# High and low parts of small operands stacked at partitions 0 and 32 of one matmul

## The chip, the core and the metric

The program runs on one core of one Trainium2 chip. The metric is device time in microseconds, the median of three runs. Engines: PE (TensorE, matmuls; PEld is its weight load), DVE (VectorE), ACT (ScalarE), POOL (GpSimd) and SP (SyncE, which only issues DMAs here).

## What is computed

One decoder layer for a prompt of 512 tokens and for 8 sample rows of one token each, in fp32. Cut to what matters here:

```python
h  = rms_norm(x, norm_g) * (1 + scale) + shift                 # modulated by c
aq, ak, av, az, mqk, mv, mo, mz, mif, ga, gm = split_columns(h @ w_in)
ya = attend(aq, ak, av)          # samples: top-3 of 8 past key blocks of a paged cache, plus the new row
# mLSTM, per head (4 heads): b = cumsum(logf), d = b_t - b_s + i_s
m_t = maximum(b + m0, max_s d)                                 # running maximum, the stabiliser
w   = exp(d - m_t);  s = (q @ k.T) * w;  num = s @ v;  C, n = new matrix memory
# samples, per row: C_new = a*C + v k^T, num = C_new q, with q, k = silu(conv(mqk))
u  = sigmoid(ga) * ((ya * silu(az)) @ w_att) + sigmoid(gm) * ((ym * silu(mz)) @ w_mlstm)
y  = rms_norm(x + gate * (u @ w_out), final_g)
```

## The kernel before

Matmuls in full fp32 are slow on PE, so the kernel splits operands into a **high part** (the value as a rounded fp32r copy) and a **low part** (the value less its high part) and multiplies with fp32r matmuls. For the large products (`ztile`, L544 to L565) a weight tile of 128 columns arrives by DMA (`wraw`), ACT makes the high part (`high`, L1022), POOL the low part (`low`, L1519), and PE runs three products for each of 8 contraction steps and 2 halves of 260 columns: high by high, high by low, low by high. A tile is 48 matmuls.

The stages in order: modulation and normalisation (to about 54 us); attention, four pairs of heads in a loop, in which SP loads the samples' key pages, DVE and POOL multiply them with spread queries and DVE sums them; the choice of blocks for the samples (about 245 to 275 us); four mLSTM heads of 8 tiles each, with value pages between; the gate tiles (`T_GATE`) with the samples' state update; the output products.

Each engine runs its own program in order; semaphores (`wait_ge`, `then_inc`) join them. Nothing is scheduled by a tool: the order is as written. Four places of the program matter below, in all of which a few rows are spread over all 128 partitions by a matmul with a selector (a stationary matrix of rows that are all ones or all zeros):

- **Query copy** (`query_copy`, L684 to L688). The samples' queries (8 rows, 512 columns) lie in `qsr`, high parts in columns 0 to 511 and low parts in the next 512, both on partitions 0 to 7. Two fp32r matmuls with the selector `selc` accumulate. ACT makes the rounded copy (L1118) and a plain copy `qsN` (L1119), POOL the difference (`query_low`, L1558). ACT copies the result out (`copy_out`, L1168), which waits in the loop until DVE has freed all pages. Eight of these, two for each pair of heads.
- **Spread of the running maxima** (`spread_max`, L763 to L767). `MR` has 4 rows (heads) of 512 tokens. One matmul of plain fp32 operands with the selector `selm` (fp32, written by ACT, L1250 and L1276) spreads one head's row; in the trace each is two rows. ACT takes exponentials of the result (`decays`, L1273 to L1278). Four of these, one per head. `MR` comes from a transposition of `ec` (L733), a copy and a scan along the tokens on DVE (L1793, L1794).
- **Spread of the samples' keys and queries** (`key_query`, L923 to L934). `kqr` holds 1024 high and 1024 low columns on partitions 0 to 7, and four fp32r matmuls per sample accumulate into two banks. It comes from transpositions of `cvS` (L899), ACT's copies (L1372, L1373, L1378) and a subtraction on DVE (L2088). DVE writes the selector `selg`. Eight samples.
- **The choice of blocks** on DVE (L1924 to L1961): first two convolutions for head 0 (L1901, L1904), then comparisons of block sums up to a penalty matrix (L1941), which PE spreads (L877), and sums that PE spreads again (L791), after which head 0's maxima are spread.

Of the kernel before, what the change touches and what calls it, by code (L numbers as in the profile page):

```python
# [87 lines left out]
def decoder_step(nc, I, O):  # L88
# [14 lines left out]
    with ExitStack() as ctx:  # L103
        names = set()

        def sb(name, shape, dt=F32):
# [121 lines left out]
        selm = work(P)[0:MH, :]  # L228
# [149 lines left out]
        def _(sp):  # L378
# [161 lines left out]
        def _(pe):  # L540
# [357 lines left out]
            for k in range(KT):  # L898
                last = tr(ps[0:B, 4 + k // 4, (k % 4) * P:(k % 4 + 1) * P], cvS[:, (k + 4) % KT, :], ident[:, :])  # L899
# [112 lines left out]
        def _(act):  # L1012
# [237 lines left out]
            f(selm, rowsel[0:MH, 0, :], ACT.Copy).then_inc(selm_rdy, 1)  # L1250
# [20 lines left out]
            def decays(h, first):  # L1271
# [4 lines left out]
                f(selm, chunk(rowsel[0:MH], h + 1), ACT.Copy).then_inc(selm_rdy, 1)  # L1276
# [81 lines left out]
            f(cvS[:, :, :], cvS[:, :, :], ACT.Silu).then_inc(sam_act, 1)  # L1358
# [336 lines left out]
        def _(dve):  # L1695
# [75 lines left out]
            def gates_in():  # L1771
# [14 lines left out]
            def gate_sums():  # L1786
                dve.wait_ge(g_pe, 1)
                chain(v.tensor_copy(bc[:, :, :].rearrange("p j h -> p (j h)"), ps[:, 7, 0:16]))
                tt(ec[:, :, :], G[:, 0:TT, 0:MH], bc[:, :, :], ALU.subtract).then_inc(g_dve, 1)

            def gate_max():
                dve.wait_ge(g_pe, 2)
                chain(v.tensor_copy(eR, ps[0:MH, 7, :]))  # L1793
# [213 lines left out]
            def samples_joined():  # L2007
# [267 lines left out]
```

## Time and profile before

| | |
|---|---|
| three runs | 717.66, 722.49, 724.09 us, median 722.49 |
| span of the profiled execution | 725.2 us (2.7 us over the median; its own time is not listed apart from its span) |
| PE busy | 687.4 us, 95% |
| POOL, DVE, ACT busy | 433.6, 472.8, 333.6 us |
| mean granted clock of PE | 0.971 |

A stretch's rows are read so: start and length in microseconds, then engine, line of the kernel, operation, output and inputs with shapes, a count where several run one behind the other, and in brackets how long the engine idled before and what ended that. A matmul's length reaches to its modelled end, so lengths of neighbouring matmuls overlap, and what one occupies is the distance between starts. The granted clock is 1.00 at 2.4 GHz and 0.50 at 1.2 GHz.

### The profile page before, as it was taken

What the parts mean: (1) busy time and instruction counts of PE and PEld (TensorE: products, weight loads), DVE (VectorE), ACT (ScalarE), POOL (GpSimd) and SP (SyncE); (2) the same over time, 40 slices, a digit from 0 to 9 for tenths busy, and PEclk for the clock granted to TensorE, in tenths of its full rate; (3) what the DMA queues carried; (4) which work ended last, traced back from release to release, by engine and by line L of the source; (5) the groups of instructions that cost most, each with busy time, mean ns of one, the idle gap of its engine ahead of it and who ended that gap; (6) DMA issues with size and microseconds to landing.
All of it is one profiled execution on the core that took longest, in us unless ns stands there. A gap on an engine that the chain in (4) does not pass through costs nothing.

```text
span 725.2 us, 14754 instructions
## 1 busy us (share of the span) xinstructions
PE 687.4 (95%) x5012; PEld 611.9 (84%) x5012; DVE 472.8 (65%) x483; ACT 333.6 (46%) x726; POOL 433.6 (60%) x289
## 2 busy tenths in 40 slices
PE   1899999999999899999999999999999999999996
PEld 0577788888779668999999999997999999999974
DVE  0535489897999963995697686775555358444435
ACT  5545556547381335464464534632322224323643
POOL 4203365596687317699679688771864657666510
PEclk9997999989999978999999999999899999999999
DMA  8988349889898867287777667766675355833302
GB/s 311 343 250 248 111 123 272 267 260 274 233 304 260 269 205 233 80 248 208 228 212 230 183 189 231 226 205 192 161 198 150 101 167 167 263 88 87 88 30 89
DMA packets 156905, 144.72 MB, mean 200 GB/s; under 512 B 7548, under 2 KB 115153, under 8 KB 156853
## 3 DMA queue, kind: packets, MB, share of 16 engines
q1 hardware_dynamic: 142984, 137.15, 63.1%
q10 hardware_dynamic: 13876, 7.02, 3.3%
q8 instruction: 23, 0.38, 0.2%
q14 instruction: 22, 0.17, 0.1%
HBM read 135.10 MB, written 9.11 MB: 199 GB/s over the span
## 4 chain that ended last, share of the span: by engine, by line
PE 62%; issue 10%; POOL 9%; DVE 8%; ACT 4%; DMA 4%; SPq 2%; ACTq 0%; POOLq 0%; DVEq 0%
PE ps L556 44%; POOL sb_arenaA L1566 4%; POOL sb_wL L1519 4%; PE ps L992 3%; PE ps L822 2%; POOL sb_arenaA L1600 1%; PE ps L932 1%; DVE sb_arenaA L1838 1%; PE ps L590 1%; PE ps L783 1%; DMA sb_arenaA<-in_w_ada 1%; DVE sb_arenaB L1986 1%; DMA sb_arenaB<-in_x_sample 1%; DVE sb_arenaA L1981 1%; SPq L398 1%
## 5 line engine op out<-in xcount | busy, mean ns | idle before, releaser
L1519 POOL TENSOR_TENSOR sb_wL<-sb_wraw,sb_wH 128x512 fp32r<-128x512 f32 (+1 forms) x168 | 217.7, 1312 | 188.5 <-ACT sb_wH L1022 170.5
L556 PE MATMUL ps<-sb_hH,sb_wH 128*128 128x260 f32 x1152 | 242.0, 292 | 3.6 <-POOL sb_wL L1519 3.0
L556 PE MATMUL ps<-sb_hH,sb_wL 128*128 128x260 f32 x1152 | 235.6, 287 | 0.0
L556 PE MATMUL ps<-sb_hL,sb_wH 128*128 128x260 f32 x1152 | 235.3, 286 | 0.0
L556 PEld LDWEIGHTS ps<-sb_hH,sb_wH 128*128 128x128 f32 x1152 | 181.7, 193 | 19.6 <-issue 14.7
L1022 ACT ACTIVATE sb_wH<-sb_wraw 128x512 fp32r<-128x512 f32 (+1 forms) x168 | 99.3, 612 | 191.1 <-PE ps L556 150.5
L556 PEld LDWEIGHTS ps<-sb_hL,sb_wH 128*128 128x128 f32 x1152 | 181.5, 193 | 0.0
L556 PEld LDWEIGHTS ps<-sb_hH,sb_wL 128*128 128x128 f32 x1152 | 181.2, 192 | 0.0
L1600 POOL TENSOR_TENSOR sb_arenaA<-sb_arenaA 128x2048 f32<-128x2048 f32 x28 | 101.5, 3628 | 2.0 <-DMA sb_arenaA<-in_cache_v 2.0
L1566 POOL TENSOR_TENSOR sb_arenaA<-sb_arenaA 128x1024 f32<-128x1024 f32 x22 | 61.7, 2823 | 35.3 <-DMA sb_arenaA<-in_cache_k 35.3
L1842 DVE TENSOR_REDUCE sb_arenaA<-sb_arenaA 128x2048 f32 (+1 forms) x32 | 73.0, 2284 | 3.7 <-DVE sb_arenaA L1838 2.0
L1838 DVE TENSOR_TENSOR sb_arenaA<-sb_arenaA 128x2048 f32<-128x2048 f32 x21 | 53.9, 2565 | 6.8 <-DMA sb_arenaA<-in_cache_k 5.8
L1981 DVE TENSOR_REDUCE sb_arenaA<-sb_arenaA 128x512 f32<-128x4096 f32 x7 | 53.6, 7656 | 0.3 <-POOL sb_arenaA L1600 0.3
L1986 DVE TENSOR_REDUCE sb_arenaA<-sb_arenaA 128x512 f32<-128x4608 f32 x4 | 34.3, 8583 | 0.0
L1027 ACT ACTIVATE sb_arenaB<-ps 128x520 f32<-128x520 f32 (+1 forms) x57 | 33.9, 594 | 0.9 <-ACT sb_kqN L1239 0.8
L1986 DVE TENSOR_REDUCE sb_arenaB<-sb_arenaA 128x512 f32<-128x4608 f32 x3 | 25.6, 8537 | 13.0 <-POOL sb_arenaA L1600 13.0
L1143 ACT ACTIVATE sb_arenaB<-ps,sb_nmx 128x512 f32<-128x512 f32 (+3 forms) x32 | 16.4, 526 | 25.0 <-DVE sb_nmx L1824 24.9
L667 PE MATMUL ps<-sb_arenaB 64*128 64x384 f32 (+3 forms) x64 | 22.9, 498 | 3.7 <-ACT sb_arenaA L1168 3.2
L2106 DVE CAST sb_kqr<-sb_rowsel 8x128 fp32r (+1 forms) x8 | 6.1, 757 | 29.8 <-PE ps L932 29.8
L590 PE MATMUL ps<-sb_arenaA,sb_gated 128*32 128x512 f32 x112 | 15.4, 670 | 10.7 <-DMA sb_arenaA<-in_w_ada 10.4
L2172 DVE TENSOR_TENSOR sb_arenaB<-ps,sb_arenaB 128x520 f32 x8 | 5.6, 700 | 30.1 <-PE ps L556 30.1
L667 PEld LDWEIGHTS ps<-sb_arenaB 64*128 64x128 f32 x64 | 10.8, 204 | 11.6 <-ACT sb_arenaB L1157 4.4
(389 smaller groups left out, 979.1 us busy)
## 6 DMA issues: line engine op xcount, KB each, us to landing
sb_wraw<-in_w_in SPq DMA_DIRECT2D x64, 512.0 KB, 5.3
sb_arenaA<-in_cache_k SPq DMA_DIRECT2D x128, 256.0 KB, 3.2
sb_arenaA<-in_cache_v SPq DMA_DIRECT2D x128, 256.0 KB, 3.2
sb_arenaA<-in_w_ada SPq DMA_DIRECT2D x6, 2048.0 KB, 11.6
sb_arenaB<-in_state_C SPq DMA_DIRECT2D x8, 512.0 KB, 4.2
sb_wraw<-in_w_mlstm SPq DMA_DIRECT2D x8, 512.0 KB, 5.3
sb_wraw<-in_w_out SPq DMA_DIRECT2D x8, 512.0 KB, 3.9
sb_arenaB<-in_x_prompt SPq DMA_DIRECT2D x1, 2048.0 KB
```

The lines of the kernel that those rows point to most:

```text
L556: last = mm(ps[:, 2 * s + a, 0:HALF], w[:, s, k, :], x[:, k, a * HALF:(a + 1) * HALF], start=(k == 0 and w is wH and x is xH), stop=(k == ...
L590: last = mm(ps[32 * g:32 * g + 32, bank, :], (hS if i == W_Q else cT)[:, k, :], ada[:, i % 2, k, :], start=(k < 4), stop=(k >= 4))
L667: last = mm(ps[:, b, c:c + (q + 1) * P], qT[r, q * P:(q + 1) * P], kT[r, 0:(q + 1) * P], start=True, stop=True)
L1022: f(wH[:, j % 2, part], wraw[:, j % 4, part], ACT.Copy).then_inc(hi_done, 1)
L1027: ins = f(halves(dst), zps(j % 2), func)
L1519: tt(wL[:, j % 2, part], wraw[:, j % 4, part], wH[:, j % 2, part].bitcast(F32), ALU.subtract)\
L1566: last = tt(two, two, qbc[:, s // 4:s // 4 + 1, :].broadcast_to([P, 2, AW]), ALU.mult)
L1600: tt(heads, heads, score[:, bass.ds((8 * h + s) * 32, 32)].unsqueeze(2).broadcast_to([P, 32, DH]), ALU.mult).then_inc(pool_mult, 1)
L1838: chain(tt(four, four, qbc[:, s // 4:s // 4 + 1, :].broadcast_to([P, STEP_PAGES, AW]), ALU.mult))
L1842: v.tensor_reduce(score[:, bass.ds((8 * t + s) * 32, 32)], page[:, s % 4, :].rearrange("p (g n) -> p g n", n=DH), AX, ALU.add)\
L1981: v.tensor_reduce(vhalf, vpairs[0], AX, ALU.add).then_inc(pair_free[0], 1)
L1986: v.tensor_reduce(vacc[e], vpairs[1], AX, ALU.add).then_inc(pair_free[1], 1)
```

## The change

The high parts of a small operand now lie on partitions 0 to 7 (0 to 3 for the maxima) and the low parts on partitions 32 to 39 (32 to 35) of the same columns. The selectors carry ones in row i and in row 32 + i, so one fp32r matmul over 40 (36) contraction rows adds both. To have the value on both sets of partitions the transpositions and sums ahead of it take operands with their columns doubled (`groupsum2`, `ec2`, `cvS2`). The low parts of the queries are made by DVE and no longer by POOL. The maxima get a rounded copy `MRr` (ACT) and a low part (DVE), which they did not have, and PE waits for it (`mr_lo`).

```diff
 def query_copy(e, t, bank):
-    mm(ps[:, bank, :], selc[:, e, :], qsr[:, 0:AW], start=True, stop=False)
-    mm(ps[:, bank, :], selc[:, e, :], qsr[:, AW:2 * AW], start=False, stop=True).then_inc(qbc_mm, 1)
+    mm(ps[:, bank, :], selc[:, e, :], qsr, start=True, stop=True).then_inc(qbc_mm, 1)
 ...
-    mm(ps[0:B, 6, :], groupsum[:, 0:B], modp[:, 0, :], start=True, stop=True).then_inc(q_mm, 1)
+    pe.wait_ge(consts, 3)
+    mm(ps[0:SROWS, 6, :], groupsum2, modp[:, 0, :], start=True, stop=True).then_inc(q_mm, 1)
 ...
-    last = tr(ps[0:MH, 7, j * P:(j + 1) * P], ec[:, j, :], ident[:, :])
+    last = tr(ps[0:MROWS, 7, j * P:(j + 1) * P], ec2[:, j, :], ident[:, :])
 ...
 def spread_max(h):
-    mm(ps[:, 7, :], selm, MR[:, :], start=True, stop=True).then_inc(mb_mm, 1)
+    pe.wait_ge(mr_lo, 1)
+    mm(ps[:, 7, :], selm, MRr, start=True, stop=True).then_inc(mb_mm, 1)
 ...
 def key_query(e, t):
     for a in range(2):
-        for part in range(2):
-            first = (2 * part + a) * AW
-            last = mm(ps[:, 4 + 2 * e + a, :], selg[:, e, :], kqr[:, first:first + AW],
-                      start=(part == 0), stop=(part == 1))
+        last = mm(ps[:, 4 + 2 * e + a, :], selg[:, e, :], kqr[:, a * AW:(a + 1) * AW], start=True, stop=True)
 ...
 # ACT
-f(selm, rowsel[0:MH, 0, :], ACT.Copy).then_inc(selm_rdy, 1)
+f(MRr, MR[:, :], ACT.Copy).then_inc(mr_hi, 1)
+f(selm, rowsel[0:MROWS, 0, :], ACT.Copy).then_inc(selm_rdy, 1)
 ...
-f(cvS[:, :, :], cvS[:, :, :], ACT.Silu).then_inc(sam_act, 1)
+f(cvS2[:, :, 0:B], cvS[:, :, :], ACT.Silu)
+f(cvS2[:, :, LOW:LOW + B], cvS[:, :, :], ACT.Silu).then_inc(sam_act, 1)
 ...
 # POOL, constants
+chain(nc.gpsimd.affine_select(out=rowsel[:, :, :], in_=rowsel[:, :, :], compare_op=ALU.not_equal, fill=1.0,
+                              base=-LOW, pattern=[[-1, B + 2], [0, P]], channel_multiplier=1))
+chain(nc.gpsimd.memset(groupsum2, 0.0))
+nc.gpsimd.tensor_copy(groupsum2[:, 0:B], groupsum[:, 0:B])
+chain(nc.gpsimd.tensor_copy(groupsum2[:, LOW:SROWS], groupsum[:, 0:B]))
+chain(nc.gpsimd.memset(ec2, 0.0))
 ...
-    pool.wait_ge(q_ev, 1)
-    tt(qsr[:, AW:2 * AW], qsN[:, :], qsr[:, 0:AW].bitcast(F32), ALU.subtract).then_inc(q_lo, 1)
 ...
 # DVE, gates
+dve.wait_ge(q_ev, 1)
+rows = slice(LOW, SROWS)
+tt(qsr[rows], qsN[rows, :], qsr[rows].bitcast(F32), ALU.subtract).then_inc(q_lo, 1)
 ...
-tt(ec[:, :, :], G[:, 0:TT, 0:MH], bc[:, :, :], ALU.subtract).then_inc(g_dve, 1)
+for dst in (ec[:, :, :], ec2[:, :, 0:MH], ec2[:, :, LOW:MROWS]):
+    last = tt(dst, G[:, 0:TT, 0:MH], bc[:, :, :], ALU.subtract)
+last.then_inc(g_dve, 1)
 ...
 # DVE, ahead of the first convolution
 dve.wait_ge(sel_act, 1)
+dve.wait_ge(mr_hi, 1)
+tt(MRr[LOW:MROWS], MR[LOW:MROWS, :], MRr[LOW:MROWS].bitcast(F32), ALU.subtract).then_inc(mr_lo, 1)
 convolve(0, 0)
 ...
 # DVE, samples_joined
-tt(cvS[:, :, :], cvS[:, :, :], cvP[:, :, :], ALU.add).then_inc(sam_dve, 1)
+v.memset(cvS2, 0.0)
+chain(tt(cvS[:, :, :], cvS[:, :, :], cvP[:, :, :], ALU.add))
+dve.sem_inc(sam_dve, 1)
 ...
-tt(kqr[:, 2 * AW:4 * AW], kqN[:, :], kqr[:, 0:2 * AW].bitcast(F32), ALU.subtract).then_inc(kq_lo, 1)
+tt(kqr[low_rows, 0:2 * AW], kqN[low_rows, :], kqr[low_rows, 0:2 * AW].bitcast(F32), ALU.subtract)\
+    .then_inc(kq_lo, 1)
```

`LOW` is 32, `SROWS` 40 and `MROWS` 36. `qsr`, `selc`, `MRr` and `selm` now share the tensor `tail`; `kqN`, `qsN`, `MR` and `rowsel` grow to 40 or 36 partitions.

On DVE, in front of the choice of blocks (`selfp` is a copy of the samples' own scores, the two rows on `ps` from `arenaB` are one convolution), before and then after:

```order
L1924 COPY sb_selfp<-ps 128x2x4x8
L1901 TENSOR_SCALAR ps<-sb_arenaB,sb_vcol 128x512
L1904 SCALAR_TENSOR_TENSOR ps<-sb_arenaB,sb_vcol,ps 128x512 x3
L1901 TENSOR_SCALAR ps<-sb_arenaB,sb_vcol 128x512
L1904 SCALAR_TENSOR_TENSOR ps<-sb_arenaB,sb_vcol,ps 128x512 x3
L1930 TENSOR_REDUCE sb_bsum<-ps 8x64
```

```order
L1939 COPY sb_selfp<-ps 128x2x4x8
L1943 TENSOR_TENSOR sb_tail<-sb_MR,sb_tail 4x512
L1916 TENSOR_SCALAR ps<-sb_arenaB,sb_vcol 128x512
L1919 SCALAR_TENSOR_TENSOR ps<-sb_arenaB,sb_vcol,ps 128x512 x3
L1916 TENSOR_SCALAR ps<-sb_arenaB,sb_vcol 128x512
L1919 SCALAR_TENSOR_TENSOR ps<-sb_arenaB,sb_vcol,ps 128x512 x3
L1947 TENSOR_REDUCE sb_bsum<-ps 8x64
```

The low part of the maxima has come in ahead of both convolutions and of everything that follows them.

On DVE in the gates (`G` the gate logits, `gf` and `lf` the forget gates, `arenaA` a page with its products), before and then after:

```order
L1776 TENSOR_TENSOR sb_G<-ps,sb_bif 8x8
L1779 TENSOR_SCALAR sb_gf<-sb_G 128x20
L1780 TENSOR_TENSOR sb_gf<-sb_gf,sb_G 128x20
L1783 SCALAR_TENSOR_TENSOR sb_lf<-sb_G,sb_gf 128x20
L1838 TENSOR_TENSOR sb_arenaA<-sb_arenaA 128x2048
```

```order
L1785 TENSOR_TENSOR sb_G<-ps,sb_bif 8x8
L1788 TENSOR_SCALAR sb_gf<-sb_G 128x20
L1789 TENSOR_TENSOR sb_gf<-sb_gf,sb_G 128x20
L1793 TENSOR_TENSOR sb_tail<-sb_qsN,sb_tail 8x512
L1796 SCALAR_TENSOR_TENSOR sb_lf<-sb_G,sb_gf 128x20
L1853 TENSOR_TENSOR sb_arenaA<-sb_arenaA 128x2048
```

The low part of the queries, which POOL made between two low parts of weights, stands here now, in front of the forget gates that wait for ACT's logarithm.

On PE, at the head of the loop over the samples (`ones` with a column is a sum of page products, the `ISA` and branch rows are waits and the loop), before and then after:

```order
L573 MATMUL ps<-sb_ones,sb_arenaB 128x1 x4
L936 UNCONDITIONAL_BRANCH
L936 ISA
L932 MATMUL ps<-sb_kqr 128x512 x4
L548 ISA
L549 ISA
L556 MATMUL ps<-sb_hH,sb_wH 128x260 x2
```

```order
L581 MATMUL ps<-sb_ones,sb_arenaB 128x1 x4
L942 UNCONDITIONAL_BRANCH
L942 ISA
L939 MATMUL ps<-sb_kqr 128x512 x2
L556 ISA
L557 ISA
L564 MATMUL ps<-sb_hH,sb_wH 128x260 x2
```

Four matmuls have become two; what stands around them is the same.

## Rows read from the trace of the kernel before

**Rows 1.** Windows, two stages: us, busy us and count by engine, granted clock, DMA, GB/s
```profile
430.00:500.00 70.00, 70.00 (x554) 66.67 (x552) 49.24 (x37) 32.98 (x69) 50.03 (x27) 1.00 0.66 195
520.00:594.00 74.00, 74.00 (x578) 70.42 (x577) 34.73 (x31) 20.68 (x36) 44.94 (x32) 1.00 0.50 140
```

**Rows 2.** Chain of waits, times of PE pieces: start us, us, engine, tile, line
```profile
270.34 2.07 PE ps L767 x2
370.88 1.05 PE ps L767 x2
528.21 1.12 PE ps L932 x4
```

**Rows 3.** Timeline, PE, one sample's four: start us, us, line, tiles, shapes, [idle before]
```profile
528.47 0.62 PE L932 MATMUL ps<-sb_kqr 8*128 8x512 f32 x2
528.94 0.38 PE L932 MATMUL ps<-sb_kqr 8*128 8x512 f32 x1
```

**Rows 4.** Groups of instructions, PE, by line: shapes, count | busy us, mean ns
```profile
L992 PE MATMUL ps<-sb_hL,sb_uH 128*128 128x512 f32 x32 | 12.5, 391 | 0.0
```

**Rows 5.** Timeline, ACT and PE, ahead of the first sample's keys
```profile
506.32 1.15 ACT L1022 ACTIVATE sb_wH<-sb_wraw 128x512 fp32r<-128x512 f32 x2 [5.00 <-DMA sb_wraw<-in_w_in]
512.34 2.04 PE L932 MATMUL ps<-sb_kqr 8*128 8x512 f32 x4 [0.61 <-DVE sb_kqr L2088]
```

**Rows 6.** Windows around two returns of the granted clock (the eighth figure)
```profile
264.00:266.00 2.00, 2.00 (x3) 0.95 (x4) 1.95 (x2) 0.00 (x0) 0.00 (x0) 0.50 0.86 259
276.00:278.00 2.00, 2.00 (x16) 2.00 (x16) 0.81 (x1) 1.16 (x3) 1.86 (x2) 0.82 1.01 320
519.00:520.00 1.00, 1.00 (x10) 1.00 (x9) 0.00 (x0) 0.39 (x1) 1.00 (x1) 0.97 0.00 0
```

**Rows 7.** Timeline, PE, the first query copy
```profile
59.62 0.49 PE L687 MATMUL ps<-sb_qsr 8*128 8x512 f32 x1
59.95 0.39 PE L688 MATMUL ps<-sb_qsr 8*128 8x512 f32 x1
```

**Rows 8.** Timeline, ACT, DVE, POOL and PE, around the choice of blocks
```profile
244.33 0.29 ACT L1250 ACTIVATE sb_arenaB<-sb_rowsel 4x128 f32<-4x128 f32 x1
247.53 0.81 DVE L1901 TENSOR_SCALAR ps<-sb_arenaB,sb_vcol 128x512 f32<-128x512 f32 x1
255.34 1.67 DVE L1937 TENSOR_TENSOR sb_scr<-sb_scr,sb_earlier 8x512 f32<-8x512 f32 x1
259.66 0.68 DVE L1941 TENSOR_TENSOR sb_scr<-sb_pen,sb_ident 8x512 f32<-8x512 f32 x1
255.04 3.12 POOL L1519 TENSOR_TENSOR sb_wL<-sb_wraw,sb_wH 128x512 fp32r<-128x512 f32 x2 [8.08 <-ACT sb_wH L1022]
260.58 1.12 PE L877 MATMUL ps<-sb_scr,sb_ones 8*128 8x512 f32 x2
```

**Rows 9.** Waits, 75 to 235 us: who waited for whom, us, times, longest
```profile
PEld ps L667 <- ACT sb_arenaB L1157: 4.4, 8, 0.8
```

**Rows 10.** Timeline, ACT and PE, two page waits of the attention stage
```profile
146.14 0.60 ACT L1168 ACTIVATE sb_arenaA<-ps 128x512 f32<-128x512 f32 x1 [4.59 <-DVE sb_arenaA L1842]
146.79 1.89 PE L667 MATMUL ps<-sb_arenaB 64*128 64x512 f32 x2 [1.59 <-ACT sb_arenaA L1168]
188.92 1.12 PE L667 MATMUL ps<-sb_arenaB 64*128 64x512 f32 x2 [1.61 <-ACT sb_arenaA L1168]
```

**Rows 11.** Timeline, POOL and DVE, the opening and the gates
```profile
27.09 4.95 POOL L1519 TENSOR_TENSOR sb_wL<-sb_wraw,sb_wH 128x512 fp32r<-128x512 f32 x4 [14.44 <-ACT sb_wH L1022]
56.86 1.27 POOL L1558 TENSOR_TENSOR sb_qsr<-sb_qsN,sb_qsr 8x512 fp32r<-8x512 f32 x1 [0.76 <-ACT sb_qsN L1119]
59.99 0.18 DVE L1783 SCALAR_TENSOR_TENSOR sb_lf<-sb_G,sb_gf 128x20 f32<-128x20 f32 x1 [1.82 <-ACT sb_gf L1125]
68.06 0.89 DVE L1819 TENSOR_TENSOR ps<-ps,sb_cmask 128x128 f32<-128x128 f32 x4 [2.02 <-PE ps L667]
```

**Rows 12.** Timeline, DVE, behind the last head's joining of the samples
```profile
480.85 1.42 DVE L2047 SCALAR_TENSOR_TENSOR ps<-ps,sb_vcol,sb_arenaB 128x512 f32<-128x512 f32 x2 [4.75 <-PE ps L840]
```

More of the change, by code:

```diff
@@ L39 @@
 MH, MQ, MV = 4, 128, 256
+LOW = 32
+SROWS, MROWS = LOW + B, LOW + MH
 PAGE, PAGES = 128, 16
@@ L173, in decoder_step @@
         yaL = sb("yaL", [P, PAIRS, NT], F32R)
-        with nc.sbuf_tensor("sb_kqr", [B, 2304], F32R) as kqr:
+        with nc.sbuf_tensor("sb_kqr", [SROWS, 1280], F32R) as kqr:
             pass
-        selg = kqr[:, 2048:2304].rearrange("p (s n) -> p s n", s=2)
+        selg = kqr[:, 1024:1280].rearrange("p (s n) -> p s n", s=2)
         uL = sb("uL", [P, KT, NT], F32R)
@@ L182, in decoder_step @@
             pass
-        sb("arenaB_rest", [P, 10620])
-        qsr = sb("qsr", [B, 1284], F32R)
-        selc = qsr[:, 1024:1280].rearrange("p (s n) -> p s n", s=2)
+        sb("arenaB_rest", [P, 10700])
+        tail = sb("tail", [SROWS, 1204], F32R)
+        qsr = tail[:, 436:948]
+        selc = tail[:, 948:1204].rearrange("p (s n) -> p s n", s=2)
+        MRr = tail[0:MROWS, 0:T]
+        selm = tail[0:MROWS, T:T + P]
         used = [0]
@@ L227, in decoder_step @@
         cout = work(3 * P)
-        selm = work(P)[0:MH, :]
         used[0] = 0
@@ L269, in decoder_step @@
         scr = sb("scr", [P, 1536])
-        eR = scr[0:MH, 0:T]
+        eR = scr[0:MROWS, 0:T]
+        groupsum2 = scr[:, 1024:1024 + SROWS]
+        ec2 = scr[:, 1072:1072 + TT * MROWS].rearrange("p (j n) -> p j n", j=TT)
+        cvS2 = scr[:, 0:KT * SROWS].rearrange("p (k n) -> p k n", k=KT)
         gT = scr[0:4 * MH, 0:NT]
-        MR = sb("MR", [MH, T])
+        MR = sb("MR", [MROWS, T])
         m0 = sb("m0", [B, MH])
@@ L737, in attention @@
                     for j in range(TT):
-                        last = tr(ps[:, 7, MH * j:MH * j + MH], MR[:, j * P:(j + 1) * P], ident[0:MH, 0:MH])
+                        last = tr(ps[:, 7, MH * j:MH * j + MH], MR[0:MH, j * P:(j + 1) * P], ident[0:MH, 0:MH])
                     last.then_inc(g_pe, 1)
@@ L898, in _ @@
             for k in range(KT):
-                last = tr(ps[0:B, 4 + k // 4, (k % 4) * P:(k % 4 + 1) * P], cvS[:, (k + 4) % KT, :], ident[:, :])
+                last = tr(ps[0:SROWS, 4 + k // 4, (k % 4) * P:(k % 4 + 1) * P], cvS2[:, (k + 4) % KT, :], ident[:, :])
             last.then_inc(sam_pe, 1)
@@ L1117, in sample_queries @@
                 act.wait_ge(q_mm, 1)
-                f(qsr[:, 0:AW], ps[0:B, 6, :], ACT.Copy)
-                f(qsN[:, :], ps[0:B, 6, :], ACT.Copy).then_inc(q_ev, 1)
+                f(qsr, ps[0:SROWS, 6, :], ACT.Copy)
+                f(qsN[:, :], ps[0:SROWS, 6, :], ACT.Copy).then_inc(q_ev, 1)
             def gate_logs():
@@ L1275, in decays @@
                     .then_inc(wsc_rdy, 1)
-                f(selm, chunk(rowsel[0:MH], h + 1), ACT.Copy).then_inc(selm_rdy, 1)
+                f(selm, chunk(rowsel[0:MROWS], h + 1), ACT.Copy).then_inc(selm_rdy, 1)
                 for k in range(TT):
@@ L1371, in _ @@
             act.wait_ge(st_misc, 16 * 5)
-            f(kqN[:, 0:AW], ps[0:B, 4, :], ACT.Copy, scale=KSCALE)
-            f(kqN[:, AW:2 * AW], ps[0:B, 5, :], ACT.Copy).then_inc(sam_act, 1)
+            f(kqN[:, 0:AW], ps[0:SROWS, 4, :], ACT.Copy, scale=KSCALE)
+            f(kqN[:, AW:2 * AW], ps[0:SROWS, 5, :], ACT.Copy).then_inc(sam_act, 1)
             high(0, T_GATE + 4, T_GATE // 4 + 1)
@@ L1788, in gate_sums @@
                 chain(v.tensor_copy(bc[:, :, :].rearrange("p j h -> p (j h)"), ps[:, 7, 0:16]))
[L1789 removed]
+                for dst in (ec[:, :, :], ec2[:, :, 0:MH], ec2[:, :, LOW:MROWS]):
+                    last = tt(dst, G[:, 0:TT, 0:MH], bc[:, :, :], ALU.subtract)
+                last.then_inc(g_dve, 1)
             def gate_max():
                 dve.wait_ge(g_pe, 2)
[L1793 removed]
+                chain(v.tensor_copy(eR, ps[0:MROWS, 7, :]))
                 v.tensor_tensor_scan(MR[:, :], eR, eR, 0.0, ALU.max, ALU.max).then_inc(g_dve, 1)
@@ L2087, in _ @@
             dve.wait_ge(sam_act, 4)
-            tt(kqr[:, 2 * AW:4 * AW], kqN[:, :], kqr[:, 0:2 * AW].bitcast(F32), ALU.subtract).then_inc(kq_lo, 1)
+            low_rows = slice(LOW, SROWS)
+            tt(kqr[low_rows, 0:2 * AW], kqN[low_rows, :], kqr[low_rows, 0:2 * AW].bitcast(F32), ALU.subtract)\
+                .then_inc(kq_lo, 1)
             dve.wait_ge(ys_ev, 1)
```

19 lines of the change are left out of this document (9 added, 10 removed).

## The prediction

> **What bounds the kernel now.** I read the kernel by stages first. From 430 to 500 us and from 520 to 594 us TensorE (PE) is busy for the whole stretch at the full granted clock of 1.00, with VectorE (DVE) and GpSimd (POOL) well below it [rows 1]. The chain of waits, read next, agrees: from the second head on it is almost only matmuls of PE, and three of its pieces are instructions that this change touches: the spreading of the running maxima (L767, 1.05 us per head from the second head on, 2.07 us for the first) and the spreading of the samples' keys and queries (L932, 1.12 us per sample) [rows 2]. So there a shorter matmul is time. The attention stage before it is different: there pages, DVE and POOL release each other, and the reader has to look at who waits for whom, below.
>
> **The halved key and query spread (L932).** Before, a sample costs four 512-column matmuls; now two. Within one sample the second starts at 528.47 and the fourth at 528.94 [rows 3], so two of the four are worth 0.47 us. That is the price with 8 contraction rows; the new ones have 40. A rounded matmul of 128 rows and 512 columns takes 391 ns from issue to end [rows 4], the fourth of L932 with 8 rows 380 ns [rows 3], so I give 40 rows the same price. Seven of the eight samples run at full clock: 7 x 0.47 = 3.29 us. The first runs at half clock: its four take 2.04 us [rows 5], two of them 1.02. The granted clock comes back only in the slice from 519 us (0.97) [rows 6], in the middle of weight matmuls. If that moment stays, what is saved ahead of it lets more of those matmuls run at half clock, and 1.02 us are worth 0.51. Sum 3.80 us. What hides none of it: DVE's reading of the banks, POOL's products and the weights all have slack from 520 to 594 us [rows 1].
>
> **The maxima as one rounded matmul (L767).** Before it is an fp32 product, in the trace two passes, 1.05 us. A single rounded 512-column matmul occupies 0.33 us: the first query copy has its two starts at 59.62 and 59.95 [rows 7]. Three heads give 3 x (1.05 - 0.33) = 2.16 us. The first head's is at half clock: 2.07 us [rows 2] against 0.51 (a quarter of the 2.04 of [rows 5]), 1.56 us less, again in front of a return of the clock: the granted clock is 0.50 from 264 us and 0.82 in the slice from 276 [rows 6].
>
> **The low part of the maxima, a new instruction on DVE.** It stands in front of the first convolution (247.53 us), with a new wait for ScalarE (ACT)'s rounded copy. That copy stands in front of the selector copy at 244.33 us, so it is done 2 to 3 us before, and the wait costs nothing; if ACT were late, the two convolutions, ACT's SiLU and all of the choice of blocks would queue behind it. The instruction itself is a 512-element two-input operation on a few partitions: 0.68 us without POOL at work, 1.67 us for a like one while POOL makes low parts of weights [rows 8]. I take 0.69, because POOL is idle for the 8.08 us ahead of 255.04 us [rows 8]. Behind it everything of the choice is late by 0.69: the last product of the block penalties now ends at 260.34 us (259.66 + 0.68) and will end at 261.03, and PE, which needs it for the matmul that starts at 260.58 [rows 8], waits 0.45 us. That comes off the first head: 1.56 - 0.45 = 1.11 us at half clock, worth 0.55 at full. The Trainium skill (SBUF — State Buffer, "Terms") says that DVE and GpSimd share a port pair under a lock held for a whole instruction, the loser blocking; the pair of prices 0.68 and 1.67 agrees. By that rule the new instruction would cost 1.67 us only if a POOL instruction overlapped it; PE would then wait 1.44 us and the sum be 0.5 us smaller.
>
> **The query copies (one matmul in place of two, eight times).** PE saves 0.33 us each, but I count nothing. The second copy of a pair is followed by scores that wait for ACT's copy out of the turned weights, eight waits of together 4.4 us [rows 9]; PE would only wait longer. The first copy of a pair is read by ACT when DVE has freed the pages: at 146.14 us ACT ends a wait of 4.59 us for DVE [rows 10]. If both covers failed, 8 x 0.33 = 2.6 us would be gained.
>
> **What moves and what is added elsewhere.** The low part of the samples' queries leaves POOL (1.27 us at 56.86) for DVE, ahead of DVE's wait for the logarithm; there DVE idles 1.82 us until 59.99 [rows 11], and a 0.68 us operation that can start when ACT's copies are done (POOL's started at 56.86) ends before PE asks for it at 59.62 [rows 7]. Behind it on DVE stand only the forget gates, for which DVE waits anyway. Without that cover PE's first copy and the gate sums would be late by up to 0.7 us. The two more subtractions of the gate sums (about 0.2 us each) lie ahead of a wait of 2.02 us that ends at 68.06 [rows 11]. POOL's longer constants (one more selection over 1280 elements, copies and two fills, some 2.5 us by their neighbours) lie in the 14.44 us in which POOL idles until 27.09 [rows 11]. The fill and the extra wait in front of the last head's joining of the samples (about 0.4 us) lie ahead of 4.75 us in which DVE waits for PE [rows 12]. ACT's copies over 40 partitions in place of 8 can take no longer than its copy of the same 512 elements over 128 partitions, 0.60 us [rows 10], and the keys' copies and the second SiLU stand ahead of ACT's 5.00 us of waiting [rows 5]. Each of these I take as nothing; all uncovered they would cost under 4 us.
>
> **Sum.** 3.80 + 2.16 + 0.55 = 6.5 us off the profiled span of 725.2 us, which gives 718.7. The median of the runs, 722.49, lies 2.7 us under that span, so I predict 722.5 - 6.5 = 716.0 us.
>
> **The rivals.** (1) The gain of the heads is given back at 507 us. ACT rounds the next weight tile only when its DMA has landed, after 5.00 us of waiting at 506.32 [rows 5], and behind it in ACT's order stands the rounding of the keys, for which PE waits until 512.34. If that landing holds its place, the 2.7 us of the heads are lost and only L932's 3.8 remain: 718.7 us. For it: ACT waits for the transfer there, so PE is not what is late. Against it: the value pages ahead of that tile are asked for when DVE has summed older pages, and DVE's sums start behind PE (DVE waits for PE at 480.85, [rows 12]), so the landing should move with PE.
> (2) A stretch of half clock more or less on PE's path. The stretch from 512.34 to 519 us is 6.6 us long and so costs 3.3. In the attention stage two waits of the same length, 1.59 and 1.61 us, end at 146.79 and 188.92; behind the first the next pair of matmuls takes 1.89 us, behind the second 1.12 [rows 10]: the same wait makes the clock fall in one case and not in the other. One such stretch less gives 712.7, one more 719.3. The Trainium skill (TensorE: Matmul & The Clock Gate, "Part 1: The HAM clock gate") says that the gate's watch runs free of the kernel's start, so that the moment of a change differs between runs; the two waits agree with it.
> (3) Slower: a rounded matmul over 40 rows is not paid like one over 8. If each took the 1.05 us of the fp32 product, a sample would cost 2.1 us in place of 1.12, eight of them 7.8 us more, the heads would gain nothing, and with the 0.45 us of the new DVE operation the time would be 730.8. It decides from 0.73 us per matmul on, where L932's loss eats the 2.7 us of the heads. For it: no rounded 512-column row of before lies between 8 and 128 rows. Against it: 380 and 391 ns at the two ends.
>
> **How the numbers follow.** Forecast 0.52, tile landing (718.7) 0.15, a stretch less (712.7) 0.16, a stretch more (719.3) 0.12, 40 rows dear (730.8) 0.05. The likeliest one's own range is 714.5 to 718: down 1.1 us if the half-clock savings count in full, and a little for the copies; up for 1.67 in place of 0.69 and for uncovered additions. The whole range takes in the neighbours, 711.5 to 721; the runs of before alone reach from 717.66 to 724.09. About 1% (7.2 us) is what a measurement here can tell from no change. Faster than 715.3: a third of the forecast and nearly all of the stretch less, 0.34. Slower by over 1%: rival 3, 0.05. Same: 0.61.
>
> **What would show it.** In the changed profile: L932's line with 16 rows and 0.65 us per sample at full clock; L767's with four rows and 0.33 us to the next start; DVE's new operation at 247 to 248 us with 0.7 us, and PE waiting about 0.45 us at the penalties' matmul; no wait for the low queries at 59 us; the attention stage unmoved. The forecast is wrong if the weight tile still lands at 506.3 us, if two spreads of keys take over 1 us at full clock, or if the half-clock stretches change in number.

## The result and the profile after

Over 20 runs each, the changed kernel took a median of 718.93 us (714.89 to 727.05) and the kernel before 725.27 us (717.66 to 729.98). The ratio is 0.9941, 95% interval [0.9921, 0.996]: faster by 0.6%, or 4.3 us, clear of no change, though under the 1% that the prediction took for what can be told here. The two medians lie 6.3 us apart and the two means 4.8 (standard error 1.0); the ratio is smaller because it leaves out each kernel's runs more than 1.5% above its fastest, three before and one after. The interval of 20 runs on each side is 0.2% to either side, not 1%.

The profiled execution has a span of 717.1 us, against 725.2 us. That difference of 8.1 us is twice the timed one, so this pair of traces can't be read off as a whole. Stage by stage it can. First the windows of the changed kernel that answer to [rows 1], and the one between them (us, busy us and count of PE, PEld, DVE, ACT and POOL, granted clock, DMA, GB/s):

```profile
430.00:500.00 70.00, 69.78 (x554) 66.12 (x557) 49.53 (x38) 33.76 (x72) 49.17 (x27) 1.00 0.67 198
500.00:520.00 20.00, 20.00 (x165) 17.05 (x158) 10.35 (x21) 8.56 (x13) 10.12 (x5) 1.00 0.92 242
520.00:594.00 74.00, 74.00 (x581) 70.36 (x580) 43.39 (x38) 21.70 (x38) 50.81 (x37) 1.00 0.54 156
```

PE is busy in the last two all the time, but from 430 to 500 us it now has 0.22 us of idle time where it had none. In the middle one it had idled for 0.61 us before, at a mean clock of 0.83:

```profile
500.00:520.00 20.00, 19.39 (x132) 15.31 (x130) 11.13 (x21) 7.80 (x12) 9.86 (x5) 0.83 0.97 252
```

The middle row now has the full clock: the stretch of half clock that ended at 519 us in the kernel before [rows 6] is not there in this execution. It was worth 3.4 us. Whether the change removed it is not shown. Before, the stretch came behind PE's wait of 0.61 us for the keys [rows 5], and DVE's subtraction, which ended that wait, had taken 2.30 us beside POOL's low parts (507.02 to 513.01 us). Now the subtraction began in a gap of POOL's (508.66 to 509.27) and took 1.22 us, and PE did not wait. Before, then after:

```profile
509.58 2.30 DVE L2088 TENSOR_TENSOR sb_kqr<-sb_kqN,sb_kqr 8x1024 fp32r<-8x1024 f32 x1
```

```profile
508.77 1.22 DVE L2108 TENSOR_TENSOR sb_kqr<-sb_kqN,sb_kqr 8x1024 fp32r<-8x1024 f32 x1
```

None of the three profiled executions of the changed kernel has the stretch. Of the ten executions of its variants below, five have one, from 508, 508, 510, 513 and 514 us: four of them behind a wait of PE at the keys (1.98, 0.55, 1.32 and 0.34 us), the one from 510 us without a wait. Two others waited there for 0.52 and 0.30 us and kept the full clock.

The spreads on PE, from the timeline (start us, us, engine, line, tiles, shapes, count, and in brackets the idle time before and what ended it):

```profile
271.37 0.50 PE L776 MATMUL ps<-sb_tail 36*128 36x512 f32 x1 [0.38 <-DVEq L1976]
308.40 0.50 PE L776 MATMUL ps<-sb_tail 36*128 36x512 f32 x1
510.78 0.73 PE L939 MATMUL ps<-sb_kqr 40*128 40x512 f32 x2
535.50 0.73 PE L939 MATMUL ps<-sb_kqr 40*128 40x512 f32 x2
572.62 0.73 PE L939 MATMUL ps<-sb_kqr 40*128 40x512 f32 x2
```

The halved instructions stand as the prediction said. From 535.50 to 572.62 us three samples take 37.12 us, 12.37 each. Before, the rows that answer to them:

```profile
540.97 1.19 PE L932 MATMUL ps<-sb_kqr 8*128 8x512 f32 x4
579.45 1.19 PE L932 MATMUL ps<-sb_kqr 8*128 8x512 f32 x4
```

That is 38.48 us, 12.83 each. So a sample gains 0.45 us. From the first sample's spread to the second's the two traces differ by more, 12.35 us (to 523.13) against 15.80 (512.34 to 528.14); most of that is the stretch of half clock.

The maxima's gain is another matter. In heads 1 to 3 no stretch of half clock falls into either trace, so they can be laid side by side. From the start of head 1's spread to the transposition that ends head 3 (L840 before, L849 after) it took 170.28 us before (309.36 to 479.64) and takes 170.36 us now. Before, then after:

```profile
309.36 1.12 PE L767 MATMUL ps<-sb_MR,sb_arenaB 4*128 4x512 f32 x2
...
479.64 1.09 PE L840 MATMUL ps<-sb_ident,sb_arenaB 128*128 128x128 f32 x8
```

```profile
308.40 0.50 PE L776 MATMUL ps<-sb_tail 36*128 36x512 f32 x1
...
478.76 1.09 PE L849 MATMUL ps<-sb_ident,sb_arenaB 128*128 128x128 f32 x8
```

Three spreads are shorter there, from 1.05 us to the next matmul before (309.36 to 310.41) to 0.43 now (308.40 to 308.83), and nothing of the 1.9 us is gained. Where most of it went shows in PE's waits from 285 to 500 us (who waited for whom: us, times, longest), before and then after:

```profile
PE ps L822 <- DVE sb_arenaB L2035: 0.5, 1, 0.5
```

```profile
PE ps L831 <- DVE sb_arenaB L2054: 1.9, 3, 1.1
```

L2054 (L2035 before) makes the weighted keys of a head. One wait of 0.5 us, in head 1, has become three, of 1.13, 0.52 and 0.22 us, one in each head. The timelines of DVE, ACT, POOL and PE in head 1 of the changed kernel show what paces them:

```profile
309.96 0.81 DVE L1916 TENSOR_SCALAR ps<-sb_arenaB,sb_vcol 128x512 f32<-128x512 f32 x1 [0.22 <-ACT sb_preS L1035]
...
316.28 0.60 ACT L1306 ACTIVATE sb_arenaB<-ps 128x512 f32<-128x512 f32 x1 [0.90 <-DVE ps L1919]
...
326.66 3.62 POOL L1609 TENSOR_TENSOR sb_arenaA<-sb_arenaA 128x2048 f32<-128x2048 f32 x1
330.24 2.54 POOL L1527 TENSOR_TENSOR sb_wL<-sb_wraw,sb_wH 128x512 fp32r<-128x512 f32 x2
...
330.32 8.51 DVE L2003 TENSOR_REDUCE sb_arenaB<-sb_arenaA 128x512 f32<-128x4608 f32 x1 [4.77 <-POOL sb_arenaA L1609]
339.04 0.69 DVE L2054 SCALAR_TENSOR_TENSOR sb_arenaB<-ps,sb_wsc 128x512 f32<-128x512 f32 x1 [0.21 <-DVE sb_arenaB L2003]
...
339.79 1.57 PE L831 MATMUL ps<-sb_arenaB 128*128 128x257 f32 x6 [1.13 <-DVE sb_arenaB L2054]
```

POOL multiplies value pages between low parts of weights, one behind the other. DVE waits 4.77 us for such a product and sums it for 8.51 us. Only behind that, in DVE's order, stand the weighted keys, and PE needs them to go on (they free the bank that its next products go to). POOL's work in a head starts from the two tiles that PE ends ahead of the spread: DVE's convolutions start when ACT has copied these tiles out (309.96), ACT waits for the convolutions (until 316.28), and only behind that does it make the next high parts, from which POOL makes the low ones. So the spread lies beside this chain and not in it; the experiments below test it.

### The profile page after: what moved, and what is told of

Same layout as the page of the kernel before. It is cut to its first block, busy times and chain, and to the rows that moved or that the text cites. A ratio compares the mean times of both kernels' runs of the same rounds, so it can differ in the third digit from the quotient of the medians.

```text
span 717.1 us, 14712 instructions
## 1 busy us (share of the span) xinstructions
PE 675.2 (94%) x4984; PEld 605.4 (84%) x4984; DVE 476.2 (66%) x488; ACT 334.8 (47%) x728; POOL 432.9 (60%) x293
## 4 chain that ended last, share of the span: by engine, by line
PE 46%; issue 15%; POOL 14%; DVE 13%; SPq 5%; DMA 3%; ACT 2%; POOLq 0%; ACTq 0%; DVEq 0%
PE ps L564 33%; POOL sb_wL L1527 6%; POOL sb_arenaA L1576 4%; POOL sb_arenaA L1609 4%; PE ps L998 3%; DVE sb_arenaA L2003 2%; DVE sb_arenaB L2003 2%; DVE sb_arenaA L1853 2%; DMA sb_arenaA<-in_w_ada 2%; SPq L406 1%; PE ps L831 1%; DVE ps L1919 1%; DVE sb_arenaA L1857 1%; SPq L407 1%; PE ps L598 1%
## 5 line engine op out<-in xcount | busy, mean ns | idle before, releaser
L1853 DVE TENSOR_TENSOR sb_arenaA<-sb_arenaA 128x2048 f32<-128x2048 f32 x21 | 56.0, 2669 | 6.8 <-DMA sb_arenaA<-in_cache_k 5.7
L2127 DVE CAST sb_kqr<-sb_rowsel 40x128 fp32r (+1 forms) x8 | 6.7, 838 | 21.8 <-PE ps L939 21.3
```

The source lines that it names most:

```text
L1853: chain(tt(four, four, qbc[:, s // 4:s // 4 + 1, :].broadcast_to([P, STEP_PAGES, AW]), ALU.mult))
```

## The experiments

Profiled executions differ by stretches of half clock, and so do the timed runs. Beside the medians I therefore give the span at the same mean clock: one common slope through span against mean granted clock within each kernel (231 runs, those over 735 us left out) is 3.8 us per 0.01, and each kernel is read at 0.975, with its standard error. The slope leans on one run of the kernel before, at a clock of 0.922; without it, it is 5.1, which leaves the 4.0 us below as they are and moves the other differences by up to 0.6 us. By that the kernel before is at 721.8 us (0.2) and the changed one at 717.8 us (0.2, 44 runs of three labels): 4.0 us less. What the change may do to the clock is left out of this; the mean clocks of the two are 0.973 and 0.974, worth about half a microsecond.

| kernel | median us | span at clock 0.975 | against the changed kernel | ratio to before |
|---|---|---|---|---|
| maxima in fp32 | 720.98 | 718.0 (0.4) | +0.2 | 0.9945 [0.9911, 0.9979] |
| keys twice (a run of 1110 us left out) | 722.3 | 721.7 (0.4) | +3.9 | 0.9976 [0.9945, 1.0007] |
| weighted keys on ACT | 718.48 | 715.1 (0.6) | -2.7 | 0.9916 [0.9872, 0.996] |
| the same, maxima in fp32 | 722.02 | 718.5 (0.6) | +0.7 | 0.9952 [0.9916, 0.9989] |
| maxima's low part on POOL | 716.74 | 716.0 (0.4) | -1.8 | 0.9907 [0.9875, 0.9939] |
| both moves, two labels | 715.1 | 714.6 (0.4) | -3.2 | 0.9879 [0.9842, 0.9915], 0.9867 [0.9825, 0.991] |
| queries twice, two labels | 719.8 | 718.4 (0.3) | +0.6 | 0.9945 [0.9913, 0.9978], 0.9902 [0.986, 0.9943] |
| both moves, queries twice | 717.96 | 715.2 (0.6) | | 0.9913 [0.9877, 0.9948] |

**The maxima undone.**

```diff
-    pe.wait_ge(mr_lo, 1)
-    mm(ps[:, 7, :], selm, MRr, start=True, stop=True).then_inc(mb_mm, 1)
+    mm(ps[:, 7, :], selm[0:MH].bitcast(F32), MR[0:MH, :], start=True, stop=True).then_inc(mb_mm, 1)
-    f(MRr, MR[:, :], ACT.Copy).then_inc(mr_hi, 1)                               # ACT
-    dve.wait_ge(mr_hi, 1)
-    tt(MRr[LOW:MROWS], MR[LOW:MROWS, :], MRr[LOW:MROWS].bitcast(F32), ...)      # DVE
```

> The changed kernel with the maxima spread as before (one fp32 matmul on the selector's and the maxima's own four rows, no rounded copy on ACT, no low part on DVE). Theory A (in heads 1 to 3 PE is paced by DVE, which sums value pages behind POOL's products and only then makes the weighted keys; the spread lies beside that): the time of the changed kernel within 1 us, ratio to before 0.993 to 0.996; PE's waits for the weighted keys in heads 1 to 3 shrink from the changed kernel's 1.13, 0.52 and 0.22 us to about 0.5, 0 and 0; the stretch from the first to the last weighted keys (282.73 to 460.49 us, 177.8 us) stays at 177.5 to 178.2 us. Theory B (the prediction's: the spread is on PE's path): 2.7 us slower than the changed kernel, ratio about 0.998, the stretch 179.4 us with the waits as they are.

Theory A held. The time at the same clock is 0.2 us over the changed kernel's (0.4), and heads 1 to 3 take 170.33 us:

```profile
306.88 1.12 PE L775 MATMUL ps<-sb_MR,sb_tail 4*128 4x512 f32 x2
...
477.21 1.09 PE L848 MATMUL ps<-sb_ident,sb_arenaB 128*128 128x128 f32 x8
```

PE's waits from 285 to 500 us are again those of the kernel before:

```profile
PE ps L830 <- DVE sb_arenaB L2050: 0.5, 1, 0.5
```

So the whole of the maxima's part, its low part included, is worth nothing that can be measured.

**The keys twice.**

```diff
-    last = mm(ps[:, 4 + 2 * e + a, :], selg[:, e, :], kqr[:, a * AW:(a + 1) * AW], start=True, stop=True)
+    for again in range(2):
+        last = mm(ps[:, 4 + 2 * e + a, :], selg[:, e, :], kqr[:, a * AW:(a + 1) * AW], start=True, stop=True)
```

> The changed kernel with each of a sample's two matmuls over 40 rows issued twice into the same bank, so that PE has four of them as before. Theory A and the prediction: 3.2 to 3.8 us slower than the changed kernel (7 x 0.45 us by the drift of the two traces per sample, and the first sample's), ratio to before 0.998 to 1.000; the distance from the second sample's spread to the last one's grows by 0.45 to 0.5 us per sample. Theory C (the gain of the samples is a shifted transfer or the clock, not the matmuls): under 1.5 us slower, ratio under 0.9965.

Slower by 3.9 us (0.4) at the same clock, as theory A and the prediction had it; the ratio, 0.9976, lies just under the range expected. In the timeline of PE:

```profile
534.30 1.19 PE L940 MATMUL ps<-sb_kqr 40*128 40x512 f32 x4
572.78 1.19 PE L940 MATMUL ps<-sb_kqr 40*128 40x512 f32 x4
```

Three samples take 38.48 us, to the hundredth what they took before with 8 rows. Here a matmul over 40 rows costs what one over 8 costs. Theory C is out, and the prediction's slower rival with it. This execution also shows the rival of the tile that lands late:

```profile
502.41 1.15 ACT L1029 ACTIVATE sb_wH<-sb_wraw 128x512 fp32r<-128x512 f32 x2 [7.64 <-DMA sb_wraw<-in_w_in]
507.15 1.15 PE L940 MATMUL ps<-sb_kqr 40*128 40x512 f32 x4 [1.98 <-DVE sb_kqr L2109]
```

ACT waited 7.64 us for a weight tile, which landed 3.0 us earlier than in the changed kernel's trace, while PE was 5.7 us ahead of that trace in the stage before; so PE then waited 1.98 us for the keys. In the changed kernel's own trace ACT's wait for that tile is 4.96 us and ends at 505.41, 0.91 us earlier than before [rows 5], with PE 0.88 us earlier: there the landing moved with PE.

**The weighted keys on ACT.** KSCALE goes into the bias of the exponent that gives `wsc`.

```diff
-    chain(f(dl[:, 0, 0:1], ps[:, 7, T - 1:T], ACT.Copy, scale=-1.0))            # ACT, decays
+    chain(f(dl[:, 0, 0:1], ps[:, 7, T - 1:T], ACT.Copy, scale=-1.0, bias=LN_KSCALE))
 ...
+    act.wait_ge(wsc_rdy, h + 1)                                                 # ACT, ahead of its wait for pv_mm
+    act.wait_ge(kt_mm, h + 1)
+    for j in range(TT):
+        last = f(kw[:, j, :], ps[:, 6, j * P:(j + 1) * P], ACT.Copy, scale=wsc[:, j:j + 1])
+    last.then_inc(kw_rdy, 1)
-    dve.wait_ge(kt_mm, h + 1)
-    dve.wait_ge(wsc_rdy, h + 1)
-    v.scalar_tensor_tensor(kw, ps[:, 6, :]..., KSCALE, over(wsc[:, :], P), ...).then_inc(kw_rdy, 1)   # DVE
```

> The changed kernel with the weighted keys of the mLSTM heads made by ACT (four scaled copies of 128 columns) ahead of its wait for the head's products, and not by DVE behind its sum of value pages. Theory A: PE's waits for the weighted keys (1.13, 0.52, 0.22 us) fall under 0.2 us in all; from the first spread of a head's maxima to the last one's (271.37 to 430.75 us, 159.4 us) it takes 1.5 to 3.5 us less unless DVE's and POOL's own sums hold it; time 1.0 to 3.0 us under the changed kernel, ratio to before 0.990 to 0.993. Theory B (PE is the bound): the waits go and nothing is gained, ratio 0.994.

```profile
306.21 0.50 PE L777 MATMUL ps<-sb_tail 36*128 36x512 f32 x1
...
328.13 8.51 DVE L2009 TENSOR_REDUCE sb_arenaB<-sb_arenaA 128x512 f32<-128x4608 f32 x1 [4.74 <-POOL sb_arenaA L1615]
...
334.10 1.14 ACT L1327 ACTIVATE sb_arenaB<-ps,sb_wsc 128x128 f32<-128x128 f32 x4
...
333.26 2.99 PE L832 MATMUL ps<-sb_arenaB 128*128 128x257 f32 x13
...
473.92 1.09 PE L850 MATMUL ps<-sb_ident,sb_arenaB 128*128 128x128 f32 x8
```

ACT makes them while DVE still sums (to 336.64 us), and PE's products run without a wait. Heads 1 to 3 take 167.71 us, 2.65 us less than in the changed kernel, and the time at the same clock is 2.7 us less (0.6). That is 0.8 us more than the three waits that went; what made up the rest is not shown. Theory A held, theory B is out: PE had been held there.

**The same with the maxima in fp32.** Both edits above.

> The changed kernel with both: the weighted keys on ACT and the maxima spread by one fp32 matmul as before. Theory A: with DVE's wait gone the spread is on PE's path, so this is slower than the kernel with the weighted keys on ACT alone by 3 x 0.55 = 1.6 us, and each head's stretch 0.5 to 0.6 us longer. Theory A2 (another link of the same chain, POOL's products and DVE's sums, paces the heads whoever makes the weighted keys): within 0.5 us of the kernel with the weighted keys on ACT alone.

```profile
312.03 1.12 PE L776 MATMUL ps<-sb_MR,sb_tail 4*128 4x512 f32 x2
...
481.56 1.09 PE L849 MATMUL ps<-sb_ident,sb_arenaB 128*128 128x128 f32 x8
```

169.53 us (312.03 to 481.56), 1.82 more than with the stacked maxima, 0.61 for each head. So the stacked spread is worth 0.61 us in a head in which PE is the bound, and nothing over three heads in which PE meets DVE. That is theory A again, and A2 is out. The timed difference is 3.3 us (0.9), more than the 1.6 expected, but within two standard errors of it.

**The changed kernel again, and the low part of the maxima on POOL.** The first is the mark on the same chip; no edit.

> The changed kernel itself, beside the next two on one chip, as the mark to which they are compared: ratio to before 0.992 to 0.996, and PE's waits for the weighted keys in heads 1 to 3 again 1.1, 0.5 and 0.2 us or within 0.3 of each (all theories).

Ratio 0.9939 [0.9906, 0.9973], and its waits for the weighted keys are again 1.9 us in three.

```diff
-    dve.wait_ge(mr_hi, 1)                                        # DVE
-    tt(MRr[LOW:MROWS], MR[LOW:MROWS, :], MRr[LOW:MROWS].bitcast(F32), ALU.subtract).then_inc(mr_lo, 1)
+    pool.wait_ge(mr_hi, 1)                                       # POOL, behind low(1, T_ML + 5)
+    pool.wait_ge(lo_done, 2 * (T_ML + 5) + 10)
+    tt(MRr[LOW:MROWS], MR[LOW:MROWS, :], MRr[LOW:MROWS].bitcast(F32), ALU.subtract).then_inc(mr_lo, 1)
+    pool.wait_ge(mr_lo, 1)
```

> The changed kernel with the low part of the maxima made by POOL, in its idle time behind the second low tile of the block (about 250 us), and not by DVE ahead of the first convolution. Theory A (the 0.7 us on DVE come on PE at the matmul that spreads the block penalties): PE's wait there falls from 1.02 us (0.98 and 0.44 in two other kernels with DVE's low part, 0.45 and 0.22 without it) to under 0.5 us, the distance from DVE's copy of the samples' own scores to its last product of the penalties (250.29 to 263.56 us, 13.27 us) falls by 0.7 us, time 0.3 to 0.8 us less, too little for the ratio to show. Theory B: POOL's operation beside DVE's convolution lengthens that by as much: the distance stays at 13.2 to 13.4 us.

First the timeline of the changed kernel, on DVE and PE:

```profile
250.29 0.28 DVE L1939 COPY sb_selfp<-ps 128x64 f32<-128x64 f32 x1 [0.31 <-DVEq L1933]
250.60 0.68 DVE L1943 TENSOR_TENSOR sb_tail<-sb_MR,sb_tail 4x512 fp32r<-4x512 f32 x1
251.31 0.81 DVE L1916 TENSOR_SCALAR ps<-sb_arenaB,sb_vcol 128x512 f32<-128x512 f32 x1
263.56 0.68 DVE L1958 TENSOR_TENSOR sb_scr<-sb_pen,sb_ident 8x512 f32<-8x512 f32 x1
...
264.30 1.12 PE L886 MATMUL ps<-sb_scr,sb_ones 8*128 8x512 f32 x2 [1.02 <-DVE sb_scr L1958]
```

Then that of the kernel with the low part on POOL:

```profile
248.97 1.28 POOL L1621 TENSOR_TENSOR sb_tail<-sb_MR,sb_tail 4x512 fp32r<-4x512 f32 x1
...
249.04 0.28 DVE L1944 COPY sb_selfp<-ps 128x64 f32<-128x64 f32 x1 [0.31 <-DVEq L1938]
249.36 0.81 DVE L1921 TENSOR_SCALAR ps<-sb_arenaB,sb_vcol 128x512 f32<-128x512 f32 x1
261.49 0.68 DVE L1961 TENSOR_TENSOR sb_scr<-sb_pen,sb_ident 8x512 f32<-8x512 f32 x1
...
262.22 1.12 PE L886 MATMUL ps<-sb_scr,sb_ones 8*128 8x512 f32 x2
```

From the copy to the last product of the penalties it is 13.27 us in the one and 12.45 in the other, and PE's wait of 1.02 us is gone. Theory A held in this trace for the distance; the wait alone would not show it, as it is 0 to 1.02 us (mean 0.57) in the seven profiled executions with DVE's low part and 0 to 0.45 (mean 0.15) in the seven without it. The timed gain of 1.8 us (0.4) is more than the 0.8 at most that was expected.

**Both moves together,** twice.

> Both moves on the changed kernel: the weighted keys on ACT and the low part of the maxima on POOL. Theory A: the 2.7 us of the one and the 0.3 to 0.8 of the other add: 3.0 to 3.5 us under the changed kernel, ratio to before 0.988 to 0.991, and PE has no wait for weighted keys. Theory B (only the key spread is worth anything): as the changed kernel, 0.994.

> The weighted keys on ACT and the low part of the maxima on POOL, again: 2.7 to 3.5 us under the changed kernel at the same mean clock, ratio to before 0.987 to 0.991. If the low part is worth nothing beside the weighted keys, 2.7 us and no more.

The two labels together are 3.2 us (0.4) under the changed kernel, and by the ratios 1.2 and 1.3% under the kernel before: the fastest version here. Heads 1 to 3 take 167.71 us again (302.05 to 469.76). Beside the weighted keys on ACT the low part's move adds only 0.5 us (0.7), and by the steeper slope nothing, so what it is worth stays open between 0 and 1.8 us.

**The query copies twice,** with the changed kernel as mark, and on both moves.

```diff
-    mm(ps[:, bank, :], selc[:, e, :], qsr, start=True, stop=True).then_inc(qbc_mm, 1)
+    mm(ps[:, bank, :], selc[:, e, :], qsr, start=True, stop=True)
+    mm(ps[:, bank, :], selc[:, e, :], qsr, start=True, stop=True).then_inc(qbc_mm, 1)
```

> The changed kernel with each of the eight query copies issued twice, so that PE has two matmuls for each as before. Theory A (the copies are covered): time within 0.7 us of the changed kernel, and PE's waits for ACT's copy of the turned weights in the attention stage (1.5 us in four waits in the changed kernel, none that PE itself had before) fall under 0.4 us, those for the pages' copy from 4.3 us to 3.2 to 4.0. Theory B (the copies are on the path): 8 x 0.33 = 2.6 us slower, with the waits unmoved.

PE's waits from 78 to 240 us, in the kernel before:

```profile
PE ps L667 <- ACT sb_arenaA L1168: 3.2, 2, 1.6
PE ps L667 <- ACT sb_arenaB L1157: 0.3, 1, 0.3
```

in the changed kernel:

```profile
PE ps L675 <- ACT sb_arenaA L1174: 4.3, 2, 2.7
PE ps L675 <- ACT sb_arenaB L1163: 1.5, 4, 0.6
```

and with the copies doubled:

```profile
PE ps L675 <- ACT sb_arenaA L1175: 3.4, 1, 3.4
PE ps L675 <- ACT sb_arenaB L1164: 0.4, 1, 0.4
```

Together 3.5 us rose to 5.8 when the copies were halved and fall to 3.8 when they are doubled again: 2.0 of the 8 x 0.33 = 2.6 us of the second copies come out of the waits, as theory A had it. But the first time the kernel was 1.3 us (0.3) over the changed one at the same clock, between the theories, so it was run again.

> The changed kernel once more, the mark for the next three on the same chip: ratio to before 0.992 to 0.996.

> The changed kernel with each of the eight query copies issued twice, again and with more rounds, because its first time stood 1.5 us over the changed kernel's at the same mean clock while its trace gave the saved matmuls back as waits. Theory A (covered): within 0.7 us of the changed kernel at the same mean clock. Theory B (partly on the path): 1.0 to 2.6 us slower again.

> The same with each query copy issued twice. Theory A (covered): within 0.7 us of the kernel without the second copies, at the same mean clock. Theory B: 1.0 to 2.6 us slower.

The changed kernel came to 0.9955 [0.9918, 0.9991]. The second time the doubled copies were at 717.5 us (0.5), 0.4 under the changed kernel; both times pooled they are 0.6 over it (0.4). On both moves they cost 0.6 (0.7). That is within theory A's bound of 0.7, and theory B's 2.6 is out; its lower end, 1.0, is one standard error away and can't be excluded.

## Why the prediction was right and wrong

It said 6.5 us off, 716.0. The ratio gives 4.3 us on the 722.49 of the three runs, and the comparison at the same clock 4.0 us (0.3). The time lies in the whole range, but above the likeliest case's own 714.5 to 718: it is that of the case with the samples' gain alone (718.7), and for another reason than the one named there. That the two medians of 20 runs lie 6.3 us apart, nearly the forecast, is luck, as a third of the forecast's sum did not come. And with 0.61 on "within 1%" the text treated as no change what 20 runs resolve as a gain.

- **Halved keys and queries, 3.80 us: right.** 0.45 us per sample for 0.47, and 3.9 us (0.4) by doubling. Taking 40 rows at the price of 8 was right too. The first sample's 0.51 us was worked out for half clock, at which it did not run in any of the three executions of the changed kernel.
- **"Three heads give 3 x (1.05 - 0.33) = 2.16 us": wrong, the step that failed.** The price was near (0.61 for 0.72; the spread occupies 0.43 us where 0.33 was taken from a query copy). What was wrong is the first paragraph's "there a shorter matmul is time". The chain of waits passes through PE from the second head on, but DVE was ready there hardly earlier than PE: the row of before with PE waiting 0.5 us for the weighted keys, shown above, was in the same trace and was not weighed. Maxima undone, weighted keys on ACT, and the two together settle it: nothing over the three heads with the weighted keys on DVE (170.33 against 170.36 us), 1.82 us with them on ACT.
- **The first head, 0.55 us: open.** DVE's low part took 0.68 us as priced, and delayed the choice by 0.82; PE waited 1.02 us for a predicted 0.45 in this execution, and 0.98, 0.85, 0.44, 0.43, 0.24 and 0 in six others with it on DVE. Half-clock stretches lie differently over this head in each trace, so its net effect was not read alone; the maxima's part as a whole is 0.2 us (0.4), which excludes neither 0.55 nor nothing.
- **Query copies as nothing: right as far as it can be told,** by waits that lengthen as the copies are halved and shorten as they are doubled. The prediction's "eight waits of together 4.4 us" [rows 9] are the weight loader's, though; PE itself had waited there for 0.3 us.
- **The moved and added work as nothing: right for the queries' low part.** DVE makes the queries' low part at 59.34 us in 0.68, and then still waits 1.81 us for the logarithm, as in [rows 11]. The other additions were not tested one by one; with 3.9 us for the keys and 4.0 in all, what is left for them and the rest of the change is 0.1 us, with an error of about half a microsecond.
- **The rivals.** The landing of the weight tile moved with PE in the traces of the changed kernel; in the execution with the keys twice it made up only 3.0 of PE's 5.7 us. The half clock differs between executions of one kernel: counted as twice what the clock lacks to 1.00, summed over windows of one microsecond, it is 43.1 us in the profiled execution before, 39.7, 43.1 and 19.5 in the three of the changed kernel, and 19.3 to 53.8 in those of the variants. The profiled pair shows the rival's one stretch less: that the one at 512 us fell away is 3.4 us of the 8.1 by which the pair differs. How often that happens in the timed runs is not shown. The dear 40 rows fell.

## What to carry to other kernels

A busy share of 100% and a chain of waits through PE don't prove that a shorter matmul is time: look in the same stage for the next engine that PE meets, and how long it waits there. In this kernel one wait of half a microsecond in one of three heads was the sign that a saving ahead of that point would come back as a longer wait, until the awaited work was moved to an engine with time to spare; that move gave more than the shorter matmul. Where stretches of half clock come and go between executions, compare stages that none of them touches, or many runs at the same mean clock.

## What the runs showed of the hardware

A POOL operation beside a DVE one did not always cost DVE time. POOL's low part at 248.97 us (1.28 us) overlaps DVE's first convolution step at 249.36, and that took 0.81 us, as it does alone in [rows 8]. DVE's two-input product at 255.34 us in [rows 8] took 1.67 us beside POOL, a like one without POOL 0.68. The operands differ: the convolution step reads one tensor in SBUF, the product reads two. DVE's subtraction of the keys, which reads two as well, took 1.22 us where it began in a gap of POOL's and 2.30 us where POOL was at work already, in the rows shown above. The Trainium skill (SBUF — State Buffer, "Who interferes with whom") states it so: a DVE instruction with at most one SBUF input, outside the modes that take both ports, does not contend with GpSimd. These rows agree as far as the number of inputs goes; whether the convolution step was outside those modes no run here shows. The prediction told the lock for DVE as a whole, which is too broad, but the instruction that it priced by it has two inputs in SBUF.
